# A fused transformer stack on one core: the first two tiles behind five norms run on x times its weight, and the cross-attention values move into the mixer

## The reference, cut to what matters

```python
def rms_norm(x, g):
    y = x * lax.rsqrt(jnp.mean(x * x, axis=-1, keepdims=True) + EPS)
    return y * g

h = rms_norm(x, norm_g[layer, 0]) * (1 + scale) + shift     # per feature
x = x + 0.5 * gate * swiglu(h, w_in, w_out)
...
k, v = jnp.split(modulate(rms_norm(x, kv_norm_g), shift, scale) @ kv_w, 2, axis=-1)
...
mem_n = rms_norm_2(mem, norm_mem_g)                          # of the memory, not of x
x = x + memory_cross_attention(rms_norm_2(x, norm_xa_g), mem_n, w_q, w_kv, w_xo)
x = x + peer_ffn(rms_norm_2(x, norm_peer_g), w_pq, subkeys, u, v)
```

## Time and profile before

| what | value |
|---|---|
| median of 3 runs | 2276.36 us (2270.97 to 2278.7) |
| profiled execution | 2279.78 us, its span 2278.0 us |
| mean granted TensorE clock | 0.918 of full |
| TensorE matmuls busy | 1996.9 us (88%) |
| VectorE busy | 1648.2 us (72%) |
| ScalarE busy | 871.6 us (38%) |
| GpSimd busy | 546.7 us (24%) |
| chain that ended last | PE 66%, DMA 22%, DVE 7%, ACT 2%, issue 2% |

### The profile page before, as it was taken

One profiled execution on the slowest core, in us unless ns is written; L12 is line 12 of the kernel. 1 busy time (PEld: TensorE's weight loads), 2 busy tenths in 40 slices (PEclk: granted clock), 3 DMA queues, 4 the chain that ended last, 5 costly groups with the idle time before them and its releaser, 6 DMA issues.

```text
span 2278.0 us, 33631 instructions
## 1 busy us (share of the span) xinstructions
PE 1996.9 (88%) x12802; PEld 1683.1 (74%) x12802; DVE 1648.2 (72%) x2885; ACT 871.6 (38%) x1388; POOL 546.7 (24%) x485
## 2 busy tenths in 40 slices
PE   6999997999999999999999998998976666766766
PEld 6999986999999998699999998988832222222222
DVE  6876876876768777354468999554898787787765
ACT  3443445444444444444445543544421121211211
POOL 0110002111101112121111001513364445445441
PEclk7999997999999998599999999998998888888888
DMA  7878751677748685045464544442899999999996
GB/s 307 312 283 332 294 217 56 240 285 253 249 165 310 266 274 215 1 148 184 147 201 152 185 167 148 167 148 93 308 422 421 421 422 421 421 422 422 421 422 257
DMA packets 88438, 602.76 MB, mean 265 GB/s; under 512 B 9875, under 2 KB 11219, under 8 KB 21244
## 3 DMA queue, kind: packets, MB, share of 16 engines
q1 hardware_dynamic: 37276, 243.46, 30.1%
q0 software_dynamic: 37120, 268.52, 28.5%
q10 hardware_dynamic: 13920, 89.15, 10.0%
HBM read 597.86 MB, written 3.16 MB: 264 GB/s over the span
## 4 chain that ended last, share of the span: by engine, by line
PE 66%; DMA 22%; DVE 7%; ACT 2%; issue 2%; ACTq 0%; SPq 0%; DVEq 0%; POOLq 0%
PE ps L745 50%; DMA row_pair<-in_peer_uv,mod_ring 21%; PE ps L776 7%; PE ps L1118 3%; DVE row_pair L2165 2%; PE ps L904 1%; PE ps L814 1%; DMA first_more<-in_ada 1%; DVE w_lo L1601 1%; DVE work L1666 1%; PE ps L927 1%; PE ps L826 1%; PE ps L906 1%; DVE root L1656 1%; ACT work L1280 0%
## 5 line engine op out<-in xcount | busy, mean ns | idle before, releaser
L1601 DVE TENSOR_TENSOR w_lo<-raw,w_hi 128x2048 fp32r<-128x2048 f32 (+1 forms) x248 | 526.0, 2122 | 258.5 <-ACT w_hi L1140 258.2
L745 PE MATMUL ps<-HH,w_hi 128*128 128x256 f32 x2160 | 614.6, 285 | 0.0
L745 PE MATMUL ps<-HL,w_hi 128*128 128x256 f32 x2160 | 611.2, 283 | 0.0
L745 PE MATMUL ps<-HH,w_lo 128*128 128x256 f32 x2160 | 611.2, 283 | 0.0
L1118 PE MATMUL ps<-row_pair,diag 128*128 128x512 f32 x768 | 433.5, 725 | 191.4 <-ACT diag L1568 191.4
L1140 ACT ACTIVATE w_hi<-raw 128x2048 fp32r<-128x2048 f32 (+1 forms) x248 | 438.9, 1770 | 287.2 <-PE ps L745 222.1
L1118 PEld LDWEIGHTS ps<-row_pair,diag 128*128 128x128 f32 x768 | 173.0, 233 | 451.3 <-ACT diag L1568 242.1
L745 PEld LDWEIGHTS ps<-HH,w_hi 128*128 128x128 f32 x2160 | 413.0, 191 | 0.3 <-issue 0.2
L745 PEld LDWEIGHTS ps<-HL,w_hi 128*128 128x128 f32 x2160 | 413.1, 191 | 0.0
L745 PEld LDWEIGHTS ps<-HH,w_lo 128*128 128x128 f32 x2160 | 413.0, 191 | 0.0
L2165 DVE SCALAR_TENSOR_TENSOR row_pair<-row_pair,HTOK 128x1024 f32<-128x1024 f32 x256 | 313.5, 1226 | 132.8 <-DMA row_pair<-in_peer_uv,mod_ring 131.2
(11 more groups left out here) (279 smaller groups left out, 2888.3 us busy)
## 6 DMA issues: line engine op xcount, KB each, us to landing
raw<-in_f_in SPq DMA_DIRECT2D x88, 1024.0 KB, 4.9
mod_ring<-in_ada ACTq DMA_DIRECT2D x74, 1024.0 KB, 6.8
raw<-in_f_out SPq DMA_DIRECT2D x64, 704.0 KB, 5.2
raw<-in_mix_a SPq DMA_DIRECT2D x16, 1024.0 KB, 4.9
raw<-in_mix_g SPq DMA_DIRECT2D x8, 1024.0 KB, 4.9
raw<-in_pq SPq DMA_DIRECT2D x8, 1024.0 KB, 4.9
first<-in_ada ACTq DMA_DIRECT2D x4, 1024.0 KB, 11.0
raw<-in_a_q SPq DMA_DIRECT2D x4, 1024.0 KB, 8.1
```

The costliest lines, as they stand in the source:

```text
L745: ins = mm(out_, ops[1] if left else ops[0], ops[0] if left else ops[1], start=(first and k == k0 and n == 0), stop=(last and k == k1 - 1 ...
L1601: v.tensor_tensor(slot(w_lo, g), slot(raw, g), f32(slot(w_hi, g)), ALU.subtract).then_inc(low["v"], 1)
```

## The change

For the five norms n2, n3, n6, N_XA and N_PEER the first two weight tiles of the next layer (`RAW_TILES = 2`) are multiplied with `X * gain` instead of the normed x. The operand's high part is made by ScalarE (`raw_high`) and its low part by VectorE (`raw_low`) chunk by chunk in the layer before, and the sum of squares (`norm_sum`) moves into the middle of the first such tile. The reciprocal root multiplies the outputs. For n2, n3 and n6 the shift enters as two more columns of the operand (`WIDE = SEQ + 2` = 258 columns), and comes out as a column that is added behind the multiplication. From the third tile on a layer runs on the normed x as before. The layout of the memory is moved apart for the wider buffers. `x_v` moves from behind `mix_out` to between `x_k1` and `mix_b`, reads the memory from `EH`/`EL`, and is taken out by ScalarE alone; the taps are spread anew, and both sums of the layer norm move one tile of `sc_out` forward. In `pq`, `head_scores(0)` and `tok_turns(0)` come behind the second tile.

The diff, cut to its core:

```diff
-        ("mix_a", 16, TILE, "ad"), ("mix_g", 8, TILE, "aa"), ("x_k1", 2, TILE, "aa"), ("mix_b", 4, TILE, "dd"),
+        ("mix_a", 16, TILE, "ad"), ("mix_g", 8, TILE, "aa"), ("x_k1", 2, TILE, "aa"), ("x_v", 4, TILE, "aa"),
+        ("mix_b", 4, TILE, "dd"),
...
-        ("x_v", 4, TILE, "ad"), ("x_q", 4, TILE, "aa"),
-        ("x_o", 4, TILE, "dd"), ("pq", 8, TILE, "aa")]
+        ("x_q", 4, TILE, "dd dd aa aa".split()), ("x_o", 4, TILE, "dd"), ("pq", 8, TILE, "dd dd aa aa aa aa aa aa".split())]
...
-TAPS_IN_A, TAPS_IN_G, TAPS_IN_K, TAPS_IN_B = 13, 9, 9, 7
+TAPS_IN_A, TAPS_IN_G, TAPS_IN_K, TAPS_IN_V, TAPS_IN_B = 13, 9, 9, 9, 3
+
+RAW_TILES = 2
+WIDE = SEQ + 2
...
# TensorE
+            def raw_tile(name, t, n, mid=None):
...
+                hi, lo = RAWS[n]
+                wide = WIDE if n in SHIFTED else SEQ
+                outs = [ps[:, OUT_BANKS[(ln.chunk0 + 2 * t + m) % BANKS], 0:wide] for m in range(2)]
...
+                for k in range(DC):
+                    if t == 0:
+                        pe.wait_ge(raw_hi, RSET[n] + k + 1)
+                    for m in range(2):
+                        for u in range(2):
+                            mm(outs[m], w[u][:, k, m * P:(m + 1) * P], hi[:, k, 0:wide], start=(k == 0 and u == 0), stop=False)
+                    if t == 0:
+                        pe.wait_ge(raw_lo, RSET[n] + k + 1)
+                    for m in range(2):
+                        last = mm(outs[m], w[0][:, k, m * P:(m + 1) * P], lo[:, k, 0:wide], start=False, stop=(k == DC - 1))
...
+                    if k == 3 and mid is not None:
+                        mid()
...
+                if raw:
+                    raw_tile(w_in, 0, raw_n, mid=lambda: norm_sum(raw_n))
+                    raw_tile(w_in, 1, raw_n)
...
+            raw_tile("s_k", 0, 3, mid=lambda: norm_sum(3))
+            raw_tile("s_k", 1, 3, mid=lambda: mod_sum(27))
...
             for t in range(4):
+                tok_tile("x_v", t)
+            for t in range(4):
                 feat_tile("mix_b", t)
             for t in range(4):
                 feat_tile("sc_out", t, new="c3")
-                if t == 1:
+                if t == 0:
...
-            pe.wait_ge(hl_ready, SET["n9"] + DC)
-            for t in range(4):
-                tok_tile("x_v", t)
-            for t in range(4):
-                feat_tile("x_q", t, new="n10")
+            raw_tile("x_q", 0, N_XA, mid=lambda: norm_sum(N_XA))
+            raw_tile("x_q", 1, N_XA)
+            for t in range(2, 4):
+                feat_tile("x_q", t, new="n10", raw=True)
...
+                    pe.wait_ge(s_ready, 2 * j + half + 1)
...
+            raw_tile("pq", 0, N_PEER, mid=lambda: norm_sum(N_PEER))
+            raw_tile("pq", 1, N_PEER)
+            head_scores(0)
+            tok_turns(0)
...
# ScalarE
+            def raw_high(n, k, ready):
+
+                g = NORMS[n][0]
+                act.wait_ge(freed["d"], ready)
+                f(RAWS[n][0][:, k, 0:SEQ], X[:, k, :], ACT.Copy,
+                  scale=gain[:, k:k + 1] if n in SHIFTED else prm[:, g + k:g + k + 1]).then_inc(raw_hi, 1)
...
+            split(LIN["f01_in"].tile0 + 2)
             norm_root(2)
             shift_high("n2", 2)
...
# VectorE
+            def raw_low(n, k):
...
+                v.scalar_tensor_tensor(lo[:, k, 0:SEQ], X[:, k, :], gk, f32(hi[:, k, 0:SEQ]), ALU.mult, ALU.subtract
+                                       ).then_inc(raw_lo, 1)
...
+                if raw:
+                    split(ln.tile0 + 3)
+                    dve.wait_ge(hl_ready, SET[{2: "n2", 6: "n6"}[raw_n]] + DC)
+                    for t in range(RAW_TILES):
+                        for m in range(2):
+                            ins = v.tensor_tensor(TX[:, 2 * t + m, 0:SEQ + 1], raw_out(w_in, 2 * t + m), rinv_one, ALU.mult)
+                        ins.then_inc(raw_scaled, 1)
...
+            split(LIN["f01_in"].tile0 + 2)
             norm(2, X, "n2", 36)
```

More of the change, by code:

```diff
@@ L150 @@
 STEP_END = {"A": 8, "B": 16, "X": 18}
-TAPS_IN_A, TAPS_IN_G, TAPS_IN_K, TAPS_IN_B = 13, 9, 9, 7
+TAPS_IN_A, TAPS_IN_G, TAPS_IN_K, TAPS_IN_V, TAPS_IN_B = 13, 9, 9, 9, 3
+RAW_TILES = 2
+WIDE = SEQ + 2
+RSET = {n: 8 * k for k, n in enumerate([2, 3, 6, N_XA, N_PEER])}
+SHIFTED = (2, 3, 6)
 BATCH = 4
@@ L275, in build_program @@
         work = place("work", WORK_AT, 14 * KF)
+        HHX = three(place("HHX", HH_AT, EXT, F32R), DC)
+        HLX = three(place("HLX", HL_AT, EXT, F32R), DC)
+        EHX = three(place("EHX", KS_AT, EXT, F32R), DC)
+        ELX = three(place("ELX", VS_AT, EXT, F32R), DC)
+        ELW = three(place("ELW", WORK_AT + 4 * KF, EXT, F32R), DC)
+        RAWS = {2: (EHX, ELX), 3: (EHX, ELX), 6: (EHX, ELX), N_XA: (HHX, HLX), N_PEER: (EHX, ELW)}
         first = place("first", WORK_AT + 6 * KF, 4 * TILE)
@@ L370, in build_program @@
         MEM = three(place("MEM", MOD_AT + TILE, DC * SEQ), DC)
+        VX = three(place("VX", MOD_AT + TILE, TT * D), TT)
         gfin = mr(D)
@@ L575, in _ @@
             ffn("f11_in", "f11_out")
-            for name in ("x_k0", "mix_a", "mix_g", "x_k1", "mix_b", "sc_out", "cf_out", "mix_out", "x_v", "x_q", "x_o", "pq"):
+            for name in ("x_k0", "mix_a", "mix_g", "x_k1", "x_v", "mix_b", "sc_out", "cf_out", "mix_out", "x_q", "x_o", "pq"):
                 tiles(name)
@@ L836, in ffn @@
                 with pe.Fori(0, 3) as i:
-                    for t in range(BODY):
-                        q = {2: 0, 5: 1}.get(t)
-                        feat_tile(w_in, t, i=i, new=new,
+                    for t in range(t0, t0 + BODY):
+                        q = {2: 0, 5: 1}.get(t - t0)
+                        feat_tile(w_in, t, i=i, new=new, raw=raw,
                                   mid=(lambda: mod_sum(ada // 2 + q, i)) if more and q is not None else None)
-                for t in range(18, 22):
-                    feat_tile(w_in, t, mid=(lambda: mod_sum(ada // 2 + 6) if more else norm_sum(N_MEM)) if t == 20 else None)
+                for t in range(18 + t0, 22):
+                    feat_tile(w_in, t, mid=(lambda: mod_sum(ada // 2 + 6)) if more and not raw and t == 20 else
+                              (lambda: norm_sum(N_MEM)) if not more and t == 21 else None)
                 lo = LIN[w_out]
@@ L857, in ffn @@
                             ).then_inc(units_done, 1)
+                    if more and raw and half == 1 and m == 0:
+                        mod_sum(ada // 2 + 6)
                     if more and half == 0 and m in (3, 5):
                         mod_sum(ada // 2 + 7 + (m - 3) // 2)
-                if more:
+                if more and nxt not in RSET:
                     norm_sum(nxt)
@@ L1466, in _ @@
                     take("x_k1", q, KTX[:, 4 + q, :])
+            for t in range(4):
+                split(LIN["x_v"].tile0 + t + 2)
+                for m in range(TT):
+                    take("x_v", 2 * t + m, VX[:, m, t * 256:(t + 1) * 256])
             def short_high(k):
@@ L1498, in _ @@
             f(HH[:, DC - 1, :], Z[:, DC - 1, :], ACT.Copy).then_inc(hh_ready, 1)
+            split(LIN["sc_out"].tile0 + 5)
             def merged_high(k):
@@ L1715, in ffn @@
                     with_mod = more and 1 <= m <= 6
+                    if more and raw and m == 1:
+                        mod_take(ada // 2 + 6)
                     if with_mod:
@@ L1999, in _ @@
             for t in range(4):
+                split(LIN["x_v"].tile0 + t + 2)
+                more_taps(TAPS_IN_V)
+            for t in range(4):
                 split(LIN["mix_b"].tile0 + t + 2)
```

304 lines of the change are left out of this document (211 added, 93 removed).

## The result

| | before | after |
|---|---|---|
| median | 2274.38 us (4 runs, 2270.97 to 2278.7) | 2237.59 us (4 runs, 2233.26 to 2242.73) |
| profiled execution, its span | 2279.78, 2278.0 | 2242.73, 2240.9 |
| mean granted clock | 0.918 | 0.923 |

The ratio is 0.9833, with a 95% interval of 0.9817 to 0.9849: 36.8 us faster. Forecast were 2240 us, and 36.6 us of gain. The number is met, but that it is met so closely is luck: by the terms of the forecast the trace shows 30.5 us, six too few, and some 7 us come from a thing that no term named.

A forecast was written before the change was run, and what follows sets the result against it. TensorE was taken to set the pace up to pq, DMA queues filled by row gathers behind it. Gains of 4.2 + 6.3 + 6.0 + 15.3 + 0.3 + 4.5 = 36.6 us off the 2276.36 median gave 2240, range 2233 to 2256.

The forecast's parts named there:

- n2: Norm ahead of f01_in: of 7.0 us lost, 4.2 gained, the rest going to added work and short waits.
- n3: Norm behind f01_out: of 8.6 us lost, 6.3 gained; the modulation sum and the sum of squares stay.
- n6: Norm behind b_o, without modulation sums: of 7.5 us lost, 6.0 gained.
- N_XA: Norm ahead of x_q: raw tiles cover it in place of x_v; 0.3 us gained, from the sums of squares.
- N_PEER: Norm ahead of pq: of 11.2 us lost, 4.5 gained, with a 3.1 us stand and 2.0 for slow clock left.
- mixer: From mix_b to cf_out: moved x_v, taps and earlier sums end the waits; of 15.9 us lost, 15.3 gained.
- Rival (e): Raw tiles: matmuls with 258 columns don't reach 0.120 us each, making the kernel slower, 2284 us; chance 0.03.
- Rival (b): Behind the norms: VectorE becomes the bound; n2, n6 and n3 give 5 instead of 16.5 us, 2251; chance 0.12.
- table load: ScalarE at n2 and n6: 1.28 us without drain; with the skill's 2.66, silu 1.4 later, sum 2.8 us smaller.
- Rival (d): Mixer only shifts its waits, mix_b stays VectorE's and cf_out waits: 8 instead of 15.3 us, 2247; chance 0.14.
- The gathers: GpSimd's row gathers behind pq: they start earlier by what TensorE gained, the seventh about 37 us earlier.
- Rival (c): The gain stops at the gathers, whose own start rules: N_PEER's 4.5 us and some more go, 2246; chance 0.07.

The follow-up runs named there:

- products_first: The changed kernel with VectorE's products of each mix_b tile ahead of its split of weights, not behind it: 2231.44 us.
- ln_sums_back: The changed kernel with the layer norm's two sums back behind the second and third sc_out tile: 2240.93 us.
- taps_back: The changed kernel with the convolution's taps shared out as before, none beside x_v and seven beside each mix_b tile: 2240.97 us.
- mixer_alone: The kernel before with only the mixer's part (x_v moved, taps 13/9/9/9/3, layer-norm sums one tile earlier): 2270.74 us, ratio 0.9978.
- copy_first: The changed kernel with ScalarE's copies of the first scores ahead of its split of pq tile 3: 2227.51 us.
- layout_only: The kernel before with only its buffers moved to the changed kernel's places: 2264.73 us, ratio 0.9951.
- turns_mid: The changed kernel with pq's first transposes in the middle of tile 2 instead of ahead of it: 2229.68 us.
- hl_aligned: The changed kernel with HH, HL, SQ and KS in their old places, VS, X and work area 64 and 128 bytes off: 2238.31 us, ratio 0.9836.
- combined_places: The changed kernel with seven edits at pq, x_q, mixer and f01_in (2223.98 us without new places), its buffers shifted further: 2215.5 us, ratio 0.9737.
- split_first: The changed kernel with VectorE's split of weights ahead of its sum of modulation weights in f01_in and f11_in: 2263.45 us.
- peer_lows_vector: The changed kernel with the last norm's eight low parts made by VectorE behind its multiplies, not by GpSimd: 2229.75 us.

## Why the prediction was right, and where it wasn't

| term of the sum | forecast | in the trace |
|---|---|---|
| n2 | 4.2 | 3.1 |
| n3 | 6.3 | 6.6 |
| n6 | 6.0 | 6.2 |
| mixer | 15.3 | 11.3 |
| N_XA | 0.3 | -0.3 |
| N_PEER | 4.5 | 3.6 |
| sum | 36.6 | 30.5 |
| matmuls' pace | none | 6.8 |

The two make 37.3, and the spans differ by 37.1. The terms are without the pace: from `mix_out` to `x_o`, for instance, it is 0.2 us less than before (73.0 to 72.8), of which half a microsecond is faster matmuls, hence the -0.3.

- *The raw tiles* did what was said. No gap behind `a_o`, `f01_out`, `b_o` and `x_o`, no slow matmuls right behind them; the 258 columns cost no more than the 0.1 us a norm that was charged. Rival (e) is out. That the norms' stands went is read from the trace; no run has the raw tiles alone, with all buffers in their old places.
- *n2.* "Tile 3 wants the bank that ScalarE's first silu frees ... a wait of 0.1" was the wrong wait: the silu was in time, and 1.1 us went at the fifth tile for `w_lo`, behind the sum of modulation weights (7.0 less 1.3, 0.1, 1.1, 1.3 and 0.1 for the matmul behind). The 1.3 for `mod_sum` came as forecast. Rival (b) in small; the lateness was gone a tile later. As to the table load, ScalarE's timeline:

```profile
416.52 1.28 ACT L1329 ACT_TABLE_LOAD   x1
418.39 0.51 ACT L1329 ACTIVATE work<-work 128x256 f32<-128x256 f32 x1 [0.59 <-DVE work L1854]
```

The load ended at 417.80, and the silu started at 418.39, when VectorE's product came; tile 3 started at 419.33 without a wait. No drain is to be seen. With the 2.66 us of the Trainium skill (ScalarE: Activation LUTs, What ACT_TABLE_LOAD costs) the silu would have ended at about 419.7, an estimate, 0.4 us behind the start of tile 3 and not the 1.4 us by which the prediction had it later: most of the drain would have lain beside the wait for VectorE.

- *The mixer* is where the sum failed: "`mix_b` needs about 4.5 us of VectorE a tile ... so `sc_out` need not wait for `mix_b`'s last products". It took 5.04 us (from 1373.22 to 1378.26), since two of its three taps take 0.97 us beside GpSimd's low parts. The trace of before had shown that too (0.97 and 0.96 at 1373.77 and 1374.66), and I priced all taps at 0.4. And VectorE began on `mix_b` 3.5 us after its first tile was done: in `x_v` it had no idle time, and could not make up for anything. So the last product stood behind a split, 3.05 us of stand and slow matmuls: 4 us. `products_first` showed the order to be the cause of the stand, though with the wait that it brings elsewhere only 1 to 2 us of the 4 come back. The rest of the step held: `ln_sums_back` puts the earlier sums at 5.4 us, `taps_back` the cover for the taps at 7.6. Rival (d) is half of it.
- *N_XA.* The raw tiles covered the norm, but the split behind ScalarE's high parts came 0.4 us late. `mixer_alone` showed what is lost without raw tiles there, 9.4 us.
- *N_PEER.* 3.6 us of stand where 3.1 were forecast, and the slow clock behind; the mechanism as told, ScalarE's split ahead of its copy (`copy_first`).
- *The gathers* shifted by what `pq` shifted. Over all fourteen traces the time from `pq`'s last matmul to the end lies between 633.2 and 638.5 us, whatever came before. Rival (c) is out.
- *The pace* was in no term, and no row of before could show it, as next to nothing there ran faster than 120 ns (5 of 380 groups). `layout_only` puts it at 11 to 12.5 us (7.3 to 14.8 by its interval) and shows it to come from the buffers' new places, a side of the change that the forecast passed over ("0.12 us (like 256) is taken"). So of the 36.8 us a third or so may be due to it; the profiled execution shows 6.8, traces of other kernels with the same places 9 to 14.

Open is what sets the pace within the same places: the mixer's matmuls (1220 to 1320) are 835 in the changed kernel and 851 in `turns_mid`, whose code up to there is the same; `f00_in`'s (70 to 170) are 840 in both and 853 in `copy_first`, where the code is the same too. One trace stands for each kernel, so how often a stage goes at either pace is not known.

```profile
1220.00:1320.00 100.00, 100.00 (x851) 1.00 0.48 178
```

That a distance to the weights of a multiple of 256 bytes is what slows them stays a guess. `hl_aligned` and `combined_places` moved the pace the way that it says, but it doesn't explain the 118.6 of `f_out`, nor two paces in the same places; which pair of buffers does it was not singled out.

## What to carry to other kernels

Where a norm stands ahead of a matrix product, the product of the unscaled input can start at once and be scaled at its output; two tiles of 5.8 us cover the chain of root, reciprocal, multiplies and split, and what then stopped TensorE here was the order of work on the engines beside it, one copy behind one split. A small job ahead of a wait can be free, and put behind it cost 26 us in `split_first`, so read what an engine waits for ahead of an instruction before moving another past it. After a change that moves buffers, count matmuls in windows of a stage that it didn't touch, before the gain is put down to the idea: here some 7 to 12 of 37 us were not the idea's.

## What the runs showed that was not expected

- The same fp32r matmuls of 256 columns, granted clock 1.00, take 120.0 or 117.7 ns, for whole stages at a time; it goes with the buffers' places (5 of 380 fast groups in the kernel before, 179 of 382 with 64 to 256 bytes of shift, 348 of 381 with other shifts), and moving seven buffers by another 64 or 128 bytes was worth 8.5 us of 2224.
- A VectorE tap or multiply with two inputs in SBUF (0.40 us each in a row) takes 0.7 to 0.88 beside a GpSimd subtraction, so low parts given to the idle GpSimd cost VectorE nearly as much as making them itself (5.7 against 3.3 + 2.8 us for eight chunks), and the high parts come 2.3 us later.
- Behind stands of 1.2 and 1.8 us (`peer_lows_vector`, `copy_first`) 48 matmuls took 5.8 us; behind 3.6 us, in the changed kernel, they took 7.5 us, with PEclk 0.50 (the 1.2 GHz level) in the window.
